# The first attention: projection tiles and attention units in one order of slots

## The reference, cut to what matters

```python
h = rmsnorm(x, g_mix[l])
proj = h @ w_in[l]
a_in, q, k, v, f_logit, gate_a, gate_b = jnp.split(proj, COL_SPLITS, axis=-1)
...
qh, kh, vh = heads(q, g_q), heads(k, g_k), heads(v, None)      # rmsnorm per head of q and k
c = jnp.cumsum(log_sigmoid(f_logit + b_forget), axis=1)
s = einsum(qi, kh) * scale + ci - c                            # per block of 128 queries
s = where(k_pos <= q_pos, s, -inf)
p = softmax(s); out = einsum(p, vh)
...
merged = sigmoid(gate_a) * y_conv + sigmoid(gate_b) * y_attn
```

## Time and profile before

| what | us |
|---|---|
| median of three runs | 3215.75 (3213.92 to 3218.97) |
| the profiled execution | 3221.1 |
| its span | 3219.6 |
| PE busy | 2889.2 (90%) |
| DVE busy | 1638.7 (51%) |
| ACT busy | 1262.6 (39%) |
| POOL busy | 298.1 (9%) |

### The profile page before, as it was taken

One profiled execution on the slowest core, in us unless ns is written; L12 is line 12 of the kernel. 1 busy time (PEld: TensorE's weight loads), 2 busy tenths in 40 slices (PEclk: granted clock), 3 DMA queues, 4 the chain that ended last, 5 costly groups with the idle time before them and its releaser, 6 DMA issues.

```text
span 3219.6 us, 38010 instructions
## 1 busy us (share of the span) xinstructions
PE 2889.2 (90%) x15328; PEld 2444.8 (76%) x15328; DVE 1638.7 (51%) x1993; ACT 1262.6 (39%) x1943; POOL 298.1 (9%) x387
## 2 busy tenths in 40 slices
PE   7999898999999999999998799977879299999994
PEld 5777787788898898988877678866768177777773
DVE  3266656542333333333333542357753578888886
ACT  3133333241232112121123312147752268777774
POOL 1001100000000000000000000013321301111102
PEclk9989888999999999999998899988989699999997
DMA  4100000111213222221231311100031589999995
GB/s 158 40 20 1 20 20 21 33 53 47 98 40 92 66 74 83 63 84 59 76 95 54 132 46 42 33 1 1 1 132 45 193 278 358 361 362 367 362 364 208
DMA packets 283326, 369.00 MB, mean 115 GB/s; under 512 B 10748, under 2 KB 169904, under 8 KB 283152
## 3 DMA queue, kind: packets, MB, share of 16 engines
q1 hardware_dynamic: 269776, 322.08, 29.9%
q0 software_dynamic: 13376, 44.48, 4.4%
HBM read 341.26 MB, written 25.26 MB: 114 GB/s over the span
## 4 chain that ended last, share of the span: by engine, by line
PE 74%; issue 12%; DVE 7%; ACT 3%; POOL 2%; DMA 2%; SPq 0%; ACTq 0%; DVEq 0%; POOLq 0%
PE ps L416 71%; DVE misc L2042 1%; ACT r L391 1%; POOL misc L821 1%; PE ps L2463 1%; PE ps L867 1%; PE ps L495 0%; DVE r L400 0%; DMA f<-in_w_in_dram 0%; PE ps L2429 0%; DVE f L2324 0%; DVE f L2619 0%; DVE f L2567 0%; DVE f L2322 0%; DVE f L2325 0%
## 5 line engine op out<-in xcount | busy, mean ns | idle before, releaser
L416 PE MATMUL ps<-r,r 128*128 128x512 f32 (+2 forms) x11952 | 2398.9, 361 | 68.5 <-DVE r L400 44.6
L416 PEld LDWEIGHTS ps<-r,r 128*128 128x128 f32 x11952 | 2019.8, 193 | 390.0 <-DVE r L400 43.4
L391 ACT ACTIVATE r<-f 128x2048 fp32r<-128x2048 f32 (+3 forms) x405 | 567.7, 1428 | 390.0 <-PE ps L416 373.9
L2387 DVE TENSOR_TENSOR r<-f,r 128x2048 fp32r<-128x2048 f32 x188 | 424.0, 2288 | 76.6 <-ACT r L391 76.5
L400 DVE TENSOR_TENSOR r<-f,r 128x1024 fp32r<-128x1024 f32 (+3 forms) x217 | 249.0, 1167 | 420.3 <-ACT r L391 420.0
L416 PE MATMUL ps<-f,f 128*128 128x128 f32 (+5 forms) x1442 | 278.2, 344 | 19.2 <-ACT f L922 14.8
L416 PEld LDWEIGHTS ps<-f,f 128*128 128x128 f32 (+2 forms) x1442 | 204.9, 213 | 57.9 <-issue 31.2
L1206 DVE TENSOR_TENSOR f<-ps,f 128x256 f32<-128x256 f32 x160 | 67.8, 424 | 241.8 <-PE ps L416 241.8
L674 DVE SCALAR_TENSOR_TENSOR f<-f,misc,f 128x1023 f32<-128x1023 f32 (+29 forms) x120 | 146.8, 1258 | 0.0
L1379 ACT ACTIVATE r<-f 128x512 fp32r<-128x512 f32 x44 | 27.8, 632 | 210.8 <-DVE f L1405 210.8
L1969 ACT ACTIVATE f<-ps,misc 128x1280 f32<-128x1280 f32 x64 | 85.2, 1331 | 63.6 <-DVE misc L2042 63.4
(11 more groups left out here) (266 smaller groups left out, 1912.3 us busy)
## 6 DMA issues: line engine op xcount, KB each, us to landing
f<-in_w_gate_dram SPq DMA_DIRECT2D x64, 1024.0 KB, 13.3
f<-in_w_up_dram SPq DMA_DIRECT2D x64, 1024.0 KB, 10.1
f<-in_w_down_dram SPq DMA_DIRECT2D x64, 1024.0 KB, 10.8
f<-in_w_in_dram SPq DMA_DIRECT2D x68, 512.0 KB, 3.9
f<-in_w_ada_dram SPq DMA_DIRECT2D x48, 512.0 KB, 3.7
f<-in_w_ffn_in_dram SPq DMA_DIRECT2D x44, 512.0 KB, 4.8
f<-in_w_ffn_out_dram SPq DMA_DIRECT2D x24, 384.0 KB, 3.3
f<-in_w_out_dram SPq DMA_DIRECT2D x16, 512.0 KB, 4.0
```

Source lines behind the costliest of these rows:

```text
L391: self.act.activation(st.hi[st.slot[i]][:, 0:n], st.raw[i % len(st.raw)][:, 0:n], ACT.Copy).then_inc(self.sem(st.name + "_hi"), 1)
L416: return self.pe.matmul(o, left, right, start=start, stop=stop, skip_group_check=True)
L2387: self.dve.tensor_tensor(es.lo[i % 4], es.raw[i % 7], es.hi[i % 4].bitcast(F32), ALU.subtract).then_inc(self.sem("e_lo"), 1)
```

## The change

The calls for each group become one loop over slots. A group has 20 slots `k`. Projection tile `k` stands in slots 0 to 7, its turn two slots later, unit `v` in slot `v + 4`; the last three steps of a group's units fall in slots 0 to 2 of the next group, and for the last group beside three gate tiles. The units come in another order. The banks are dealt anew: projection tiles and scores share banks 0 to 3 by the parity of the group, the turned tiles use banks 5 and 7. The copy of v on ACT now waits for the normalising on DVE. DVE adds two taps in slots 0 to 7 and one in each other slot (28 a group, where there were 25). The waits on whole groups become waits on single tiles. The gate tiles use bank `(n + 2) % 4`. Some semaphores are shared in other rows.

```diff
+    UNITS = [(0, 0), (0, 1), (1, 0), (1, 1), (4, 0), (2, 0), (4, 1), (2, 1),
+             (5, 0), (3, 0), (5, 1), (3, 1), (6, 0), (7, 0), (6, 1), (7, 1)]
+    PAIR_OF = {0: 0, 1: 1, 4: 2, 2: 3, 5: 4, 3: 5, 6: 6, 7: 7}
+    SLOTS = 20
+    def wide_before(self, g, u):
+        return 8 * g + sum(i >= 4 for i, _ in self.UNITS[:u])
+    def slots(self):
+        for s in range(4 * self.SLOTS + 3):
+            g, k = s // self.SLOTS, s % self.SLOTS
+            if k >= 4 and g < 4:
+                yield g, k, g, k - 4
+            elif k < 3 and g:
+                yield g, k, g - 1, self.SLOTS + k - 4
+            else:
+                yield g, k, None, None
+    def score_base(self, g):
+        return 2 * (g % 2)
+    def project_bank(self, g, t):
+        sb = self.score_base(g)
+        pb = 2 - sb
+        return (pb, pb + 1, sb, sb + 1, pb, pb + 1, pb, pb + 1)[t]
+    def scores_of(self, g, u):
+        sb, kw = self.score_base(g), (self.UNITS[u][0] + 1) * P
+        b0 = sb + u % 2 if u < 4 else (sb if u % 2 == 0 else 2 - sb)
+        return b0, self.ps[:, b0:b0 + 1 + (kw > 512), :].rearrange("p a b -> p (a b)")[:, 0:kw]
+    def pe_attention(self):
+        for g, k, ga, v in self.slots():
+            if g < 4 and k < 8:
+                if k == 0:
+                    for q in range(3):
+                        self.operand(self.ws, self.i_pj + 3 * g + q)
+                self.pe_project(g, k)
+                if g == 0 and k == 1:
+                    self.pe_cumulate()
+            if g < 4 and 2 <= k < 10:
+                self.pe_turn_qk(g, k - 2)
+            if g == 4:
+                self.pe_gate_tile(k)
+            if v is not None:
+                if v < 16:
+                    self.pe_scores(ga, v)
+                if 3 <= v and self.UNITS[v - 3][1] == 1:
+                    self.pe_turn_o(ga, v - 3)
+                if 2 <= v < 18:
+                    self.pe_values(ga, v - 2)
+                if 1 <= v < 17:
+                    self.pe_turn_p(ga, v - 1)
+    def act_attention(self):
+        self.high(self.ws, self.i_pj + 3)
+        for g, k, ga, v in self.slots():
+            if g < 4 and k < 8:
+                self.act_squares(g, k)
+            if g < 4 and 2 <= k < 10:
+                self.act_turn_qk(g, k - 2)
+            if g == 4:
+                self.act_gate_tile(k)
+            if v is not None:
+                if v < 16:
+                    self.act_exp(ga, v)
+                if 3 <= v and self.UNITS[v - 3][1] == 1:
+                    self.act_copy_o(ga, v - 3)
+                if 1 <= v < 17:
+                    self.act_copy_p(ga, v - 1)
+            if g < 4 and 1 <= k < 8:
+                if k == 1:
+                    self.act_values(g, 0)
+                self.act_values(g, k)
+            if g < 4 and k in (10, 12, 14):
+                self.high(self.ws, self.i_pj + 3 * (g + 1) + (k - 10) // 2 + 1)
+    def dve_attention(self):
+        self.low(self.ws, self.i_pj + 3)
+        for g, k, ga, v in self.slots():
+            if g == 0 and k == 1:
+                self.dve_cumulate()
+            if g < 4 and k < 8:
+                self.dve_mean_squares(g, k)
+            if v is not None:
+                if v < 16:
+                    self.dve_largest(ga, v)
+            if g < 4 and k < 8:
+                self.dve_normed(g, k)
+            if v is not None:
+                if 2 <= v < 18:
+                    self.dve_scale(ga, v - 2)
+                if 1 <= v < 17:
+                    self.dve_copy_p(ga, v - 1)
+            if g < 4:
+                self.dve_taps(2 if k < 8 else 1)
+            if g < 4 and k in (10, 12, 14):
+                self.low(self.ws, self.i_pj + 3 * (g + 1) + (k - 10) // 2 + 1)
...
+    def pe_project(self, g, t):
         pe, sem, ps = self.pe, self.sem, self.ps
+        if t in (0, 1):
+            if g:
+                pe.wait_ge(*sem("at_exp", 16 * g - 1))
+            else:
+                pe.wait_ge(*sem("glu", 5 + t))
+                pe.wait_ge(*sem("fg_d", 1))
+        elif t in (2, 3):
+            if g:
+                pe.wait_ge(*sem("at_exp", 16 * g))
+            else:
+                pe.wait_ge(*sem("fgT", t - 1))
+        else:
+            before = 8 * g + (t - 4 if t < 6 else t - 2) + 1
+            pe.wait_ge(*sem("pj_nrm", before))
+            pe.wait_ge(*sem("pj_v", before))
         w = lambda k: (self.parts[:, :, k * P:(k + 1) * P], self.parts[:, :, 1024 + k * P:1024 + (k + 1) * P])
+        for k in range(8):
+            m = self.mm3(ps[:, self.project_bank(g, t), 0:384],
+                         (self.HT[0][:, k, t * P:(t + 1) * P], self.HT[1][:, k, t * P:(t + 1) * P]), w(k), k == 0, k == 7)
+        m.then_inc(sem("pj_mm"), 1)
+
...
+    def act_values(self, g, t):
+        self.act.wait_ge(*self.sem("pj_nrm", 8 * g + t + 1))
         if g:
+            self.act.wait_ge(*self.sem("at_pv", 16 * g))
+        self.act.copy(self.VV[:, t, :], self.segments(g, t)[2]).then_inc(self.sem("pj_v"), 1)
...
+    def turn_bank(self, t):
+        return 7 if t % 2 else 5
+    def pe_turn_qk(self, g, t):
         pe, sem, ps = self.pe, self.sem, self.ps
+        if t == 7:
+            pe.wait_ge(*sem("at_ot", 8 * g + 1))
+        if t >= 2:
+            pe.wait_ge(*sem("qk_ev", 8 * g + t - 1))
+        elif t == 1:
+            if g:
+                pe.wait_ge(*sem("at_ot", 8 * g))
+            else:
+                pe.wait_ge(*sem("cc", 2))
+        elif g:
+            pe.wait_ge(*sem("at_ptd", 8 * g))
+        else:
+            pe.wait_ge(*sem("glu_sig", 8))
+        pe.wait_ge(*sem("pj_aug", 8 * g + t + 1))
+        pe.wait_ge(*sem("pj_nrm", 8 * g + t + 1))
+        for q in range(4):
+            m = pe.transpose(ps[0:66, self.turn_bank(t), q * P:(q + 1) * P], self.QK[t % 2][:, q, :], self.ident)
+        m.then_inc(sem("qk_T"), 1)
...
+    def pe_scores(self, g, u):
+        pe, sem = self.pe, self.sem
+        i, h = self.UNITS[u]
+        kw = (i + 1) * P
+        b0, _ = self.scores_of(g, u)
+        pe.wait_ge(*sem("qk_ev", 8 * g + i + 1))
+        if u < 2:
+            pe.wait_ge(*sem("pj_nrm", 8 * g + u + 3))
+            pe.wait_ge(*sem("pj_v", 8 * g + u + 3))
+        elif u < 4:
+            pe.wait_ge(*sem("at_exp", 16 * g + u - 1))
+        elif u == 4:
+            pe.wait_ge(*sem("at_exp", 16 * g + 4))
+        elif u == 5:
+            pe.wait_ge(*sem("pj_nrm", 8 * g + 8))
+            pe.wait_ge(*sem("pj_v", 8 * g + 8))
+        else:
+            pe.wait_ge(*sem("at_exp", 16 * g + u - 1))
...
+    def pe_turn_o(self, g, u):
+        pe, sem = self.pe, self.sem
+        pair = 8 * g + self.PAIR_OF[self.UNITS[u][0]]
+        pe.wait_ge(*sem("at_om", 16 * g + u + 1))
+        if pair:
+            pe.wait_ge(*sem("at_ot", pair))
+        pe.wait_ge(*sem("qk_ev", 8 * g + (6 if pair % 8 == 0 else 8)))
+        pe.transpose(self.ps[:, 7, 0:P], self.OM[pair % 2], self.ident).then_inc(sem("at_oT"), 1)
...
+    def pe_gate_tile(self, n):
+        pe, sem = self.pe, self.sem
+        mt, hf, b = n // 2, n % 2, (n + 2) % 4
+        (w,) = self.operand(self.ws, self.i_ga + mt)
+        if n >= 4:
+            pe.wait_ge(*sem("ga", n - 3))
+        else:
+            pe.wait_ge(*sem("at_exp", 63 + n // 2))
...
```

More of the change, by code:

```diff
@@ L751, in act_project @@
[L751 to L769, removed]
@@ L785, in dve_project @@
[L785 to L802, removed]
-            for q, src in ((0, pq), (1, pk)):
-                t = dve.tensor_tensor(
-                    self.QK[j][:, 2 * q:2 * q + 2, 0:64], src.rearrange("p (h d) -> p h d", h=2),
-                    self.iv4[j][:, 2 * q:2 * q + 2].rearrange("p (h o) -> p h o", o=1).to_broadcast([P, 2, 64]),
-                    ALU.mult)
-            t.then_inc(sem("pj_nrm"), 1)
-            self.dve_taps(2)
@@ new lines, in segments, with act_squares @@
+    def segments(self, g, t):
+        slots = [self.ws.slot[self.i_pj + 3 * g + q] for q in range(3)]
+        return [self.ps[:, self.project_bank(g, t), s * P:(s + 1) * P] for s in slots]
+    def act_squares(self, g, t):
+        act, sem = self.act, self.sem
+        pq, pk, _ = self.segments(g, t)
+        n, j = 8 * g + t, t % 2
+        act.wait_ge(*sem("pj_mm", n + 1))
+        if n >= 2:
+            act.wait_ge(*sem("pj_st", n - 1))
+        act.activation(self.SQ[j][:, 0:P], pq, ACT.Square)
+        act.activation(self.SQ[j][:, P:2 * P], pk, ACT.Square).then_inc(sem("pj_sq"), 1)
@@ L818, in pool_project @@
+    def pool_project(self):
+        pool, sem = self.pool, self.sem
+        for n in range(4 * NT):
+            g, t = n // NT, n % NT
+            j = t % 2
             pool.wait_ge(*sem("pj_ms", n + 1))
@@ new lines, in pe_scores @@
+    def pe_scores(self, g, u):
[16 more added lines that the diff above has]
+            pe.wait_ge(*sem("at_exp", 16 * g + u - 1))
+        for c0 in range(0, kw, 512):
+            w = min(512, kw - c0)
+            diag = c0 + w == kw
```

(29 more changed lines are left out.)

370 lines of the change are left out of this document (140 added, 230 removed).

## The result

The changed kernel takes 3239.07 us (median of four runs, 3237.32 to 3264.51), the kernel before 3215.73 (four runs): ratio 1.0092, with a 95% interval of 1.005 to 1.0133. It is slower by 23 us, where 3188 was predicted and at most 3214. The profiled execution is the slowest of the four: 3264.51 us, 43.4 more than that of before.

A forecast was written before the change was run, and what follows sets the result against it. PE was taken as the bound, with time won only where it idles or runs slowly. Four groups of 90.4 us save 56 us of 417.9, less 28 for clock losses: 3188 us, range 3155 to 3214.

The forecast's parts named there:

- What is bound, and what could be won: Head-group stage: 80.4 us of PE work a group, so 96 of 417.9 us are idle or low clock and can be won.
- What goes: Start of the units: three PE gaps, 5.7 us in all, and the gaps at a group's end go.
- What is late next: Slot 9: PE idles 3.2 us for ACT's output copy behind DVE's taps, plus 0.6 us for an exponential, in every group.
- Slots 10 to 15: Larger units: late DVE work and the copy of P keep PE's values waiting 6.2 us a group.
- The clock: After the slot 9 gap: clock lost in three groups of four, 9.3 us a loss, 28 us in all.
- four cases: Kernel before: low-clock stretches of 23.8, 13.6, 44.3 and 20.4 us, whose mean of 25.5 us was taken for the new gap.
- second rival: From slot 9: clock lost until the next group's projection, 28 us a group, 112 in all, 3272 us; chance 0.08.
- three of four: Slot 9 gap: each group given four chances in five of losing the clock, counted as three groups of four.
- Third rival: Slots 10 to 15: short gaps beside values make all four groups lose the clock again, 54 us, 3214 us; chance 0.12.

The follow-up runs named there:

- e7: e4_both with the high and low parts of the next weights made in slots 16 to 18 instead of 10, 12 and 14, taps moved to the gate tiles; 3135.62 us.
- e4_both: Changed kernel with ACT copying the first output ahead of unit 4's exponential and two DVE taps moved from slot 7 to slot 19; 3151.49 us.
- e1_fill: Changed kernel with twelve added 512-column matmuls in slot 9 of each group, ahead of the turn of tile 7; 3176.56 us.
- p2_large_first: Changed kernel with units 8 to 15 reordered to 7, 3, 7, 3, 6, 5, 6, 5, gap and work the same; 3209.33 us.
- p1_burst: Changed kernel with 24 added 512-column matmuls in slot 13, ahead of the scores of unit 9, gap kept; 3206.16 us.
- e3: Changed kernel with two DVE taps moved from slot 7 to slot 19; 3172.40 us.
- e2: Changed kernel with ACT copying the first output ahead of the exponential of unit 4 in slot 8; 3195.43 us.
- s1_before_filled: Kernel before with 14 added 512-column matmuls in each group, ahead of the turn of tile 7; 3202.00 us.
- e5: e4_both with DVE's tap left out of slots 10, 12 and 14, the taps following beside the gate tiles and in the gate stage; 3152.90 us.

## Why the prediction was wrong

- *What is bound, and what could be won*: right. A group's work was put at 80.4 us; PE is busy for 81.9 of 83.4 in `e7`.
- *What goes*: right. Behind the start of the stage there is no wait inside slots 0 to 8 above 0.37 us.
- *What is late next*: right in place, chain and nearly in size. PE idles from 4.7 to 7.4 us after tile 7, where 4.5 to 7.8 was predicted; the waits are 2.68 and 0.37 us, where 3.2 and 0.6 were predicted.
- *Slots 10 to 15*: right in kind, too large. 6.2 us a group were predicted; `e4_both` waits 5.5 and 2.3 us there in all four groups, 2 a group. At full clock the changed kernel's group would be 87.6 us (`e1_fill`, whose added matmuls stand for the gap), not 90.4. This error made the forecast 11 us too slow in the sum, and hides a part of the next.
- *The clock*: this step failed, in one term. "How long it then stays low the trace tells only by its four cases, 25.5 us in the mean" priced a loss at 9.3 us. In the profiled execution a low stretch was 68.3 us and a loss cost 116.1 - 87.6 = 28.5 us, and it happened in four groups, not three: 4 x 28.5 = 114 us, where 28 was predicted. Put into the sum, 3221.1 - (417.9 - 4 x 87.6) + 114 = 3268, and that execution took 3264.5. As the 28.5 is taken from the same windows, this shows only that nothing else of size is missing.
- This is the second rival: its price of 28 us a group, and its reason that only units stand behind the gap, with the largest last. It had a chance of 0.08. Its 3272 is near the profiled execution, not near the median of 3239.
- A slip in the same term: 12.8 us of work is half of 25.5 us, but the earlier trace rows have PE busy for 92.8 of the 102.1 us, which is 11.6 us of work a stretch. With it a loss would have been 10.8 us: nothing that saves the forecast.
- Why the four cases didn't carry over: in the kernel before, the units right behind the gap were 0, 7, 0, 7, in the changed one 4, 2, 4, 2, 5, 3. A duration measured behind one sequence of work was used for another. `p2_large_first` shows that the sequence matters, and `p1_burst` that 24 long matmuls do what the units didn't. The row of group 2 (44.3 us, with PE busy for 41.85) had shown that PE can be busy nearly throughout and the clock stay low all the same.
- The median lies 25 us below the profiled execution. The other three have a mean clock of 0.93 for its 0.919, which makes about 450 us at half clock for 527 (an estimate from clock and span). If that difference lies in the stage, they lost the clock for long in about three groups of four. No such execution was profiled. So the forecast's three of four may be right for the median; the price of each isn't.
- *Third rival* (it swings in slots 10 to 15): not seen in the changed kernel, which was low there already, but real. Falls behind waits of 0.8 to 0.9 us in these slots are what remained in `e1`, `e3` and `e4`.

What exactly brings the clock back stays open. The six stretches that lasted over 60 us (four in the changed kernel, one each in `e2` and `p2`) all ended at a projection or gate tile; among units it came back now and then.

## What to carry to other kernels

When an order of work is changed, look not only for what waits but for what stands behind the longest remaining wait of TensorE: if it is short matmuls (here 64-column values, scores and transposes), the clock lost in a gap of 2.7 us may not come back until the next stretch of long ones. So put long matmuls behind a wait that can't be avoided. Look also at what an instruction stands behind on its own engine: two taps later on DVE and one copy earlier on ACT were worth more here (88 us) than the overlap of two stages. Where the clock is in doubt, put a dozen matmuls with unused output into the gap. One run then tells whether the clock is lost there; for the reason, shorten the gap too, since such matmuls change two things.

## What was unexpected

- A fall can precede the end of a short gap: in the changed kernel PE went idle at 186.03, and the clock was low from 187.6, 1.1 us before PE went on. Waits of 0.8 to 0.9 us have also stood right ahead of a fall, and more often stood there without one.
- The losses repeat: in the changed kernel four stretches of 68.3 us, each group 116.0 to 116.1 us behind the last; in `s1_before_filled` eight of 13.7 and 6.8 us; in `e5` four of 37.5 us, 102.4 us apart. It may be that a group that loses the clock at its start meets the next one under the same conditions, so that one chance decides for four groups. This reading was not tested, and `e1` to `e4` speak against it as a rule: with the same waits in each group, the clock fell in only one to three groups of four. The changed kernel's executions differ by 27 us (3237 to 3264), those of before by 5.
